# Filter transforms of a Hyena block, times split by their rest modulo 4 and frequencies taken in mirrored pairs

## The reference, cut to what matters

```python
h = jnp.sin(freq[0] * (feats @ w1 + b1))
h = jnp.sin(freq[1] * (h @ w2 + b2))
h = (h @ w3 + b3).reshape(length, HY_ORDER, 2, HY_WIDTH)      # 1024, 2, 2, 512
h = h * jnp.exp(-t * deltas)[:, None, None, :]
fwd, bwd = h[:, :, 0], h[:, :, 1]
k = jnp.concatenate([fwd, jnp.zeros((1,) + fwd.shape[1:], f32), bwd[:0:-1]], axis=0)
k = k / jnp.sum(jnp.abs(k), axis=0, keepdims=True)
return jnp.fft.rfft(k, axis=0)
```

## Time and profile before

| what | value |
|---|---|
| median of 3 runs | 2636.35 us (2634.43 to 2640.3) |
| the profiled execution's own time | 2633.13 us |
| its span, first to last instruction | 2631.3 us |
| PE busy, share of span | 2414.7 us, 92% |
| DVE busy | 1917.5 us, 73% |
| ACT busy | 1320.3 us, 50% |
| POOL busy | 354.8 us, 13% |
| mean granted clock of PE | 0.960 of 2.4 GHz |
| `prepare`, from the start to the first instruction of `mix` | 272.4 us |

### The profile page before, as it was taken

One profiled execution on the slowest core, in us unless ns is written; L12 is line 12 of the kernel. 1 busy time (PEld: TensorE's weight loads), 2 busy tenths in 40 slices (PEclk: granted clock), 3 DMA queues, 4 the chain that ended last, 5 costly groups with the idle time before them and its releaser, 6 DMA issues. The chain is left out here.

```text
span 2631.3 us, 28205 instructions
## 1 busy us (share of the span) xinstructions
PE 2414.7 (92%) x11074; PEld 1814.6 (69%) x11074; DVE 1917.5 (73%) x1402; ACT 1320.3 (50%) x801; POOL 354.8 (13%) x187
## 2 busy tenths in 40 slices
PE   7899388999999894899999999999999999999994
PEld 2334367786444583688888888888888888888883
DVE  4655368863746446788888888888888888888885
ACT  2111422221001221676776776777777777677673
POOL 0443210000000200010220220221121021022010
PEclk9899689999999996899999999999999999999997
DMA  7552423444444225699999999999999999999994
GB/s 270 195 225 114 138 91 83 117 131 175 181 143 160 73 89 223 223 377 371 371 380 370 376 376 371 377 369 378 374 364 379 375 368 375 376 370 378 369 372 173
DMA packets 197759, 724.82 MB, mean 275 GB/s; under 512 B 13874, under 2 KB 59858, under 8 KB 176645
## 3 DMA queue, kind: packets, MB, share of 16 engines
q1 hardware_dynamic: 190878, 698.22, 70.4%
q0 software_dynamic: 5184, 20.97, 3.0%
q10 hardware_dynamic: 1640, 4.85, 0.5%
HBM read 676.83 MB, written 47.17 MB: 275 GB/s over the span
## 5 line engine op out<-in xcount | busy, mean ns | idle before, releaser
L2095 DVE TENSOR_TENSOR w_low<-w_raw,w_high 128x4096 fp32r<-128x4096 f32 (+2 forms) x288 | 1164.0, 4065 | 92.6 <-ACT w_high L2060 92.6
L2060 ACT ACTIVATE w_high<-w_raw 128x4096 fp32r<-128x4096 f32 (+2 forms) x288 | 964.2, 3349 | 469.2 <-PE psum L2030 259.1
L2028 PE MATMUL psum<-w_high,x_high 128*128 128x512 f32 (+1 forms) x1536 | 577.5, 376 | 20.1 <-DVE w_low L2095 17.5
L2029 PE MATMUL psum<-w_low,x_high 128*128 128x512 f32 (+1 forms) x1536 | 572.9, 373 | 0.0
L2030 PE MATMUL psum<-w_high,x_low 128*128 128x512 f32 (+1 forms) x1536 | 571.5, 372 | 0.0
L2028 PEld LDWEIGHTS psum<-w_high,x_high 128*128 128x128 f32 x1536 | 289.7, 189 | 80.8 <-DVE w_low L2095 25.2
L2030 PEld LDWEIGHTS psum<-w_high,x_low 128*128 128x128 f32 x1536 | 288.8, 188 | 52.1
L2029 PEld LDWEIGHTS psum<-w_low,x_high 128*128 128x128 f32 x1536 | 289.4, 188 | 49.6
L2041 PE MATMUL psum<-w_high,a_high 128*128 128x512 f32 x704 | 220.8, 395 | 0.0
L2041 PE MATMUL psum<-w_low,a_high 128*128 128x512 f32 x704 | 217.3, 390 | 0.0
L2041 PE MATMUL psum<-w_high,a_low 128*128 128x512 f32 x704 | 217.0, 389 | 0.0
(11 more groups left out here) (332 smaller groups left out, 2718.2 us busy)
## 6 DMA issues: line engine op xcount, KB each, us to landing
w_raw<-in_ex_w_down SPq DMA_DIRECT2D x80, 2048.0 KB, 9.6
w_raw<-in_ex_w_gate SPq DMA_DIRECT2D x64, 2048.0 KB, 9.9
w_raw<-in_ex_w_up SPq DMA_DIRECT2D x64, 2048.0 KB, 10.5
w_raw<-in_ex_w_gate SPq DMA_DIRECT2D x32, 1536.0 KB, 10.8
w_raw<-in_ex_w_up SPq DMA_DIRECT2D x32, 1536.0 KB, 7.6
arena<-in_mod_w SPq DMA_DIRECT2D x24, 1024.0 KB, 6.9
w_raw<-in_ex_w_down SPq DMA_DIRECT2D x16, 1024.0 KB, 8.8
arena<-const_dft_filter SPq DMA_DIRECT2D x8, 1024.0 KB, 6.4
```

Of the source, the lines that this page charges most:

```text
L2028: nc.tensor.matmul(o, xt_h[:, x], h[:, f], start=kk == 0, stop=False)
L2029: nc.tensor.matmul(o, xt_h[:, x], l[:, f], start=False, stop=False)
L2060: nc.scalar.activation(high[n % NHI][:, 0:w], raw[n % NS][:, 0:w], ACT.Copy).then_inc(hi_done, 1)
L2095: nc.vector.tensor_tensor(low[n % NS][:, 0:w], raw[n % NS][:, 0:w], high[n % NHI][:, 0:w].bitcast(F32), ALU.subtract).then_inc(lo_done, 1)
```

## The change

Each filter is transformed in 12 steps in place of 4 groups of two halves. Times are split by their rest modulo 4 (each rest has two blocks of 128 rows), and the frequencies 0 to 255 are paired with their mirror images 511 to 256. A step is four products. Steps 0 to 2 of six are sines, 3 to 5 cosines, for 128 frequencies; six steps give the spectra of 128 frequencies and of their 128 mirror frequencies. A step of the first kind (0, 3) fills banks 0 and 1 with the sums over the rests 0 and 2; ACT copies bank 1 and DVE forms their sum and difference in SBUF (`even`); a step of the other two kinds accumulates the rests 1 and 3 in one bank (2 or 3), and DVE adds it to and subtracts it from `even`'s result (`odd`). `spec` gets a second buffer for the last pair, a matrix load is 0.75 MiB in place of 1, and `spec_out(i)` stores two times 1 MiB after each sixth step. The orders on all engines are written anew; quarter 2 stands after step 16.

```diff
-    f = np.arange(HALF, dtype=np.float64)
+    low = np.arange(HALF // 2, dtype=np.float64)
+    f = np.concatenate([low, HALF - 1 - low])
...
-    spec = k.at(48, 16).rearrange("p (s a c) -> p s a c", s=2, a=4)
+    spec = [k.at(48, 16).rearrange("p (s a c) -> p s a c", s=2, a=4)] * 3 + [k.at(84, 16).rearrange("p (s a c) -> p s a c", s=2, a=4)]
+    even_p, even_m = ([k.at(at, 2) for at in ats] for ats in ((72, 76), (74, 78)))
...
# SP
+            def dft(h):
+                if h >= 2:
+                    sp.wait_ge(dmm, 3 * (h - 2) + 3)
+                sp.dma_start(ring[:, h % 2, 0:1536], k.c["dft_filter"][h % 4].rearrange("p m k n -> p (m k n)")).then_inc(dgot[h % 2], 16)
+            def spec_out(i):
+                order, g = divmod(i, 2)
+                sp.wait_ge(done, 6 * i + 6)
+                for s in (1, 0):
+                    sp.dma_start(k.spec_d[order, 2 * s + g], spec[i][:, s].rearrange("p a c -> p (a c)")).then_inc(sput[s], 16)
...
# PE
+            def step(i):
+                h, s = i // 3, i % 6
+                pe.wait_ge(dgot[h % 2], 16 * (h // 2 + 1))
+                if i >= 3:
+                    pe.wait_ge(done, i - 2)
+                m = ring[:, h % 2, 0:1536].rearrange("p (m k n) -> p m k n", m=6, k=2)
+                seq = sd[:, 0 if s >= 3 else 1]
+                for b in range(2):
+                    r = 2 * b + (1 if s % 3 else 0)
+                    o = ps[:, 1 + s % 3 if s % 3 else b, :]
+                    for kk in range(2):
+                        last = nc.tensor.matmul(o, m[:, 2 * (s % 3) + b, kk, :], seq[:, 2 * r + kk, :],
+                                                start=kk == 0 and (b == 0 or s % 3 == 0), stop=kk == 1 and (b == 1 or s % 3 == 0))
+                last.then_inc(dmm, 1)
...
+            step(0)
+            row_sums(0, 7)
+            unit(10)
+            step(1)
             column_sums(0)
+            unit(11)
+            step(2)
             pe.wait_ge(sdr, 1)
+            units_at = {3: 12, 4: 13, 6: 14, 7: 15, 9: 16, 10: 17}
+            for i in range(3, 12):
+                step(i)
+                if i in units_at:
+                    unit(units_at[i])
+                if i % 6 == 5:
+                    quarter(i // 6)
...
+            step(12)
+            row_sums(1, 7)
+            step(13)
             column_sums(1)
+            step(14)
             pe.wait_ge(sdr, 2)
+            step(15)
+            step(16)
+            quarter(2)
+            for i in range(17, 24):
+                step(i)
+            quarter(3)
# ACT
+            def half_of(i):
                 act.wait_ge(dmm, i + 1)
+                if i >= 6:
+                    act.wait_ge(done, i - 5)
+                nc.scalar.activation(half[:, (i // 3) % 2, :], ps[:, 1, :], ACT.Copy).then_inc(cp, 1)
# DVE
+            def even(i):
+                h = i // 3
+                dve.wait_ge(cp, h + 1)
+                if h % 2:
+                    dve.wait_ge(summed, 8 * (i // 12) + 7)
+                tt(even_p[h % 2], ps[:, 0, :], half[:, h % 2, :], ALU.add)
+                tt(even_m[h % 2], ps[:, 0, :], half[:, h % 2, :], ALU.subtract).then_inc(done, 1)
+                dve.wait_ge(done, i + 1)
+
+            def odd(i):
+                group, s = i // 6, i % 6
+                dve.wait_ge(dmm, i + 1)
+                o, b = spec[group][:, (s + 2) % 3], ps[:, 1 + s % 3, :]
+                if group in (1, 2) and s < 3:
+                    dve.wait_ge(sput[s - 1], 16 * group)
+                if s == 1:
+                    tt(o[:, 1, :], b, even_p[0], ALU.add)
+                    tt(o[:, 3, :], b, even_p[0], ALU.subtract).then_inc(done, 1)
...
+                dve.wait_ge(done, i + 1)
...
+            even(0)
             add_bias_tap(0)
+            odd(1)
+            odd(2)
             states_table(0, 0)
+            even(3)
             states_table(0, 1)
             diagonals(0)
+            odd(4)
+            odd(5)
+            even(6)
             states_table(1, 0)
```

More of the change, by code:

```diff
@@ L62, in ang @@
         return [2 * np.pi * np.outer(2 * tp + par + shift, f + 0.5) / (2 * SEQ) for par in range(2)]
-    even, odd = ang(0.0)
-    out["dft_filter"] = blocks([np.cos(even), np.cos(odd), np.sin(even), np.sin(odd)])
+    quarter = [2 * np.pi * np.outer(4 * low + r, low + 0.5) / (2 * SEQ) for r in range(4)]
+    cos, sin = ([fn(a) for a in quarter] for fn in (np.cos, np.sin))
+    mats = np.stack([sin[0], sin[2], sin[1], sin[3], cos[1], -cos[3], cos[0], cos[2], cos[1], cos[3], sin[1], -sin[3]])
+    mats = mats.reshape(2, 6, 2, P, 2, P).transpose(4, 0, 3, 1, 2, 5)
+    out["dft_filter"] = np.ascontiguousarray(mats.reshape(4, P, 6, 2, P)).astype(np.float32)
     even, odd = ang(0.5)
@@ L329, in _ @@
             bias(2)
[L330 to L336, removed]
+            unit(13)
+            dft(2)
+            unit(14)
+            unit(15)
+            dft(3)
+            unit(16)
+            spec_out(0)
+            unit(17)
+            unit(18)
             row_out(1)
             dft(4)
+            unit(19)
+            unit(20)
             dft(5)
-            for u in range(20, NU):
+            spec_out(1)
+            for u in range(21, NU):
                 unit(u)
@@ L343, in _ @@
             row_out(2)
[L344 to L347, removed]
+            dft(6)
+            dft(7)
+            spec_out(2)
+            spec_out(3)
             for s in range(2):
@@ L509, in _ @@
             pe.wait_ge(colsd, 3)
-            sines(0, lambda: row_sums(0, 7))
+            step(0)
+            row_sums(0, 7)
+            unit(10)
+            step(1)
             column_sums(0)
-            unit(10)
+            unit(11)
+            step(2)
             pe.wait_ge(sdr, 1)
[L514 to L523, removed]
+            units_at = {3: 12, 4: 13, 6: 14, 7: 15, 9: 16, 10: 17}
[5 more added lines that the diff above has]
+                    quarter(i // 6)
+            pe.wait_ge(done, 12)
             pe.wait_ge(sev, 10)
@@ L812, in _ @@
             states_table(2, 0)
+            even(12)
             add_bias_tap(1)
[L814 removed]
+            odd(13)
+            odd(14)
             states_table(2, 1)
[L816 removed]
             diagonals(2)
[L818 to L819 removed]
+            even(15)
+            odd(16)
+            odd(17)
             states_table(3, 0)
[L821 removed]
+            even(18)
+            odd(19)
+            odd(20)
             states_table(3, 1)
[L823 removed]
+            even(21)
+            odd(22)
             diagonals(3)
[L825 to L826 removed]
+            odd(23)
 def mix(k):
```

84 lines of the change are left out of this document (27 added, 57 removed).

## The result

| | before | changed | difference |
|---|---|---|---|
| median, us | 2635.39 (4 runs, 2631.94 to 2640.3) | 2599.48 (4 runs, 2595.14 to 2601.48) | −35.9 |
| ratio, 95% interval | | 0.986 [0.984, 0.9881] | |
| profiled execution, span | 2631.3 | 2593.4 | −37.9 |

A forecast was written before the change was run, and what follows sets the result against it. The prediction took PE's own work to set the pace in both transforms. Its terms −27.7 − 2.4 + 1.0 + 1.0 + 2.1 gave −26.0 us, from a median of 2636.35 to 2610.4 us, range 2603 to 2621.

The forecast's parts named there:

- Products, −27.7: PE in both filters' transforms: 48 products in place of 64 for each filter, 32 fewer at 0.867 us, −27.7 us.
- Bias tap, −2.4: PE ahead of the cosines: waits of 0.83 and 1.54 us for `add_bias_tap` covered by a whole step, −2.4 us.
- The wait of 3.46 us, +1.0: First filter: PE's wait for the second `combine` goes; one of 4.5 us for DVE's table comes ahead of `quarter(0)`, +1.0 us.
- The clock behind that wait, +1.0: PE behind the new wait at `quarter(0)`: lower clock loses as before (difference 0) or more (3.3); +1.0 us taken.
- DVE, ACT, POOL at 0: PE hides DVE's 16 more operations (9.6 us); nobody waits for ACT's copies; POOL's tables hidden with 4 us to spare: 0.
- The pair of operations at 107.28 and 107.88: DVE rows cited to show that operations with one operand in PSUM follow 0.60 us apart even while POOL works.
- Rival 2: DVE becomes the pace, its additions feeling POOL at 0.9 us more each: gain 14.4, time 2622 us; chance 0.05.
- Transfers, +2.1: End of the stage: both MiB of the last pair stored at once, 2.7 us more but starting earlier, +2.1 us; bounds 0 and 2.7.
- Rival 1: Turn of the filters: `spec_out(1)` delays a weight block by up to 5.4 us: gain 20.6, time 2615.8 us; chance 0.08.
- I move them as a block: Stages behind the barrier: no dependence on their start time was read, so they shift unchanged.
- The range: Whole kernel: 2603 to 2621 us, from the forecast's bounds 2605.9 and 2616.6 and the spread of runs before.
- The rule on the clock gate: PE: shorter bursts with waits between can send the clock down at each wait; by it every new wait is paid twice.

The follow-up runs named there:

- e3: Changed kernel with every first product of a bank done twice, 64 products for each filter again; 2626.55 us, ratio to before 0.9976.
- e5: Changed kernel with the first S5 quarter and its weight block behind step 6 in place of ahead of it; 2601.9 us, ratio 0.9884.
- e12: Changed kernel with first quarter behind step 6, weight blocks 16 and 17 behind steps 10 and 11, three unused products in the row blocks; 2593.98 us, 0.9841.
- e15: Changed kernel with first quarter behind step 6, weight blocks 16 and 17 a step later, filled row blocks, measured again; 2596.61 us, 0.9866.
- e11: Changed kernel with first quarter behind step 6 and weight blocks 16 and 17 behind steps 10 and 11; 2597.76 us, ratio 0.9865.
- e1: Kernel before, unchanged, measured and profiled a second time; 2631.52 us, ratio 0.9997.
- e4: Kernel before with the last of the four products of every sum left out, 48 products for each filter; 2605.99 us, ratio 0.9893.
- e8: Changed kernel, unchanged, measured once more; 2601.75 us, ratio 0.9876.
- e9: Kernel before with POOL's third table started only after all eight row blocks of order 1; 2628.58 us, ratio 0.9981.
- e6: Kernel before with three unused products put ahead of the first row sums of order 1; 2633.33 us, ratio 0.9997.
- the candidate: Changed kernel with first quarter behind step 6, weight blocks 16 and 17 a step later, filled row blocks; median 2595.4 us over 12 runs.

## Why the prediction was wrong, step by step

- **Products, −27.7:** right. 192 records took 86.3 us against the 87 forecast; e3 gave back 13.6 us for 13.9 in the filter where nothing else is late.
- **Bias tap, −2.4:** right. Filter 2 took 52.4 us in all four profiles of the changed kernel, −15.4 as forecast. No cosine step waited.
- **The wait of 3.46 us, +1.0:** right in place and about in size. It stood ahead of the first quarter, for DVE's table, with 4.73 us against the 4.5 taken. e5 showed what the prediction did not ask: what would be late behind it.
- **The clock behind that wait, +1.0:** the sign was wrong. The clock fell as it had (0.71 from 106 to 108 us, 0.50 from 108 to 110), but what then ran were the small products of the quarter. From its first transpose to the next step the first quarter took 4.8 us, against 4.0 for a quarter at the upper clock before: 0.8 us lost, where 1.7 us were lost before, so −0.9 in place of +1.0. That is more than the 1.0 by which filter 1 came out shorter than forecast (67.4 against 68.4); the longer wait and the next item took some of it back.
- **DVE, ACT, POOL at 0:** right in filter 2. The pair of operations at 107.28 and 107.88 that was to show PSUM operands beside POOL shows it not, since POOL's table had ended at 106.35. Another pair of the same profile does, in the row blocks, and the reading itself was right:

```profile
166.02 1.81 POOL L253 TENSOR_SCALAR arena<-arena 128x512 f32<-128x512 f32 x1
...
166.40 0.68 DVE L644 TENSOR_TENSOR arena<-psum,arena 128x512 f32<-128x512 f32 x1
167.00 0.67 DVE L645 TENSOR_TENSOR arena<-psum,arena 128x512 f32<-128x512 f32 x1
```

  In filter 1 DVE was nearer to the pace than I said: 0.42 us at weight block 16, and 3.6 as soon as PE came 4 us earlier (e5). Rival 2 had the right engine and far too high a price.
- **Transfers, +2.1:** right in three profiles, 10.1 against 7.8 us. In the result's profile the tail took 8.2, 1.7 us less than forecast: `mix` began 1.9 us behind the end of the full transfers, and 3.7 us behind it in the three others; why, no run shows. Rival 1 (late weight blocks at the turn) did not show in the changed kernel.
- **"I move them as a block", and the row blocks taken at 37.7 us:** this is the step that failed. The prediction read the fall of the clock in the earlier trace rows and used it only as a bound for another place; its sum has no term for the row blocks, nor for anything else outside the filters and the tail, and gives no reason why the clock should fall there again. In the profiles the forecast was −26.0 us and the result −37.9. Of the 11.9 us between them 9.0 lie in unchanged code (3.3 ahead of the transform, 3.9 in the row blocks, 1.8 from `mix` to the end), 1.1 in filter 1 and 1.7 in the tail. `mix` began at 236.3 us, where the prediction had about 246. Three of four profiles of the changed kernel have no fall in the row blocks: 33.8 us. The row blocks and the stretch ahead of the transform depend on the clock from one execution to the next: before itself took 78.0 and 75.6 us up to the first product, e12 82.5 and e15, with the same code there, 74.5.
- **The range** was then too narrow for the same reason. It had terms for every cost of the change and the 1.9 and 4 us by which three runs of before spread. The changed kernel spreads over 14 us, and so does before with 72 runs (2627.5 to 2641.0); a median of four runs of the changed kernel came out anywhere from 2599.5 to 2606.7. Two of the four measurements lie inside 2603 to 2621, two outside; the median of all 18 runs, 2602.6, lies just under it.
- **The rule on the clock gate** in the Trainium skill (TensorE: Matmul & The Clock Gate, "HAM oscillation — how this bites in real kernels"), weighed as speaking against the change, came true once in the first filter, behind the wait of 4.73 us, and did not repeat at each step: in filter 2 all 96 records ran at the upper level.

How the gain divides: the four profiles of the changed kernel are on average 34.1 us shorter than the two of before, of which 27.3 lie in the filters and the tail, 2.9 in the row blocks (33.8, 33.8, 37.7, 33.8 against 37.65), 1.9 ahead of the transform and 2.0 behind the barrier. The medians of all runs lie 31 apart, which leaves about 4 for the last three parts together, if the filters were as long in the executions without a profile. Whether these 4 belong to the change or to a lucky sample of profiles stays open: e3, e5 and e11 share the row blocks' code with the changed kernel and took 38.9, 36.0 and 35.8 us there, while before, e1 and e4 took 37.6 or 37.7 each time.

## What to carry to other kernels

Where an engine's rows follow each other without idle, removed work of a known row is worth nearly its full duration (13.6 and 12.8 of 13.9 us here), and what is left to find is the engine that is next behind it: walk its list up to the next wait, for the change and for a few microseconds more. Look at stretches of unchanged code in two profiles before calling them fixed: where the granted clock fell in one profile, the length was a draw here and not a constant. A range for a small change needs the spread of medians of such draws, which three runs of one kernel do not show.

## What the runs showed of the hardware that was not expected

- A DVE operation on two SBUF operands took 0.69 us when it started in the gap between two POOL operations and 1.62 when it started with one; the next took 1.75 either way. The one that came second ended 0.55 us behind the end of the first: DVE at 148.36 behind POOL at 147.81 in the result's profile, at 147.79 behind 147.23 in e8's. Operations of DVE that read PSUM took 0.69 at most beside POOL in `prepare`, in all profiles.
- The length of a gap of PE did not tell whether the granted clock would fall. It fell to 0.50 behind a stretch of 4 us in which PE was busy 2.3 with no gap over 1.7 us, and once behind a gap of 0.90 us (both in e9); the same gap of 0.90 us did nothing in the result's profile (173.93). It did not fall behind single gaps of 2.66 us (three profiles), nor behind 3.43 us in e9 and 3.45 us in e6, where before had lost 1.7 us behind 3.46:

```profile
107.67 7.13 PE L424 MATMUL psum<-arena 128*128 128x512 f32 x16 [3.45 <-DVE arena L680]
```

- Filling an idle stretch of PE with unused products went with row blocks of 33.2 and 34.2 us in the changed kernel, and its 8 runs stayed within 5.2 us; with the candidate's order the 12 filled runs spread over 15 us (2590.5 to 2605.8). The same filling gained nothing in the kernel before, whose clock fell in other places instead.
